# A hybrid streaming trunk: the SSD time-step chain laid token by token on 128 partitions, with the first B tile projected ahead of the time steps

## The reference

```python
h = rmsnorm(x, g_pre)
proj = jnp.einsum('bld,de->ble', h, w_in)          # 5648 columns; the last 16 are dt_raw
u, v, za, zb, xbc, dt_raw = jnp.split(proj, EVEN_SPLITS, axis=-1)
...
xbc, new_ctx = causal_dwconv(xbc, conv_ctx, conv_w, conv_b)   # 4 taps
xbc = jax.nn.silu(xbc)                              # 1024 columns x, 256 B, 256 C
dt = jax.nn.softplus(dt_raw + dt_bias)              # 16 heads
a = -jnp.exp(a_log)
acs = jnp.cumsum(dt * a, axis=2)                    # restarts in every block of 128 tokens
...
decay = jnp.exp(jnp.where(causal[:, :, None, None], seg, -jnp.inf))   # seg = acs_l - acs_s
to_end = jnp.exp(acs[:, :, -1:] - acs)
blk_decay = jnp.exp(acs[:, :, -1])
y_state = jnp.einsum('bclgn,bcgrpn,bclgr->bclgrp', cm, s_prev, jnp.exp(acs))
```

## Time and profile before

| | us |
|---|---|
| median of three runs | 1663.06 |
| the profiled execution | 1661.99 |
| its span, first to last instruction | 1660.2 |
| TensorE busy | 1576.7 (95%) |
| VectorE busy | 813.7 (49%) |
| ScalarE busy | 668.9 (40%) |
| GpSimd busy | 440.5 (27%) |
| mean granted TensorE clock | 0.984 of full speed |

### The profile page before, as it was taken

How to read it: one execution, slowest core, us unless ns; L and a number is a source line. 1 busy time by engine, 2 the same in 40 slices (tenths; PEclk the granted TensorE clock), 3 DMA queues, 4 the chain that set the end, 5 groups by cost and what they waited for, 6 DMA issues and landing times.

```text
span 1660.2 us, 26649 instructions
## 1 busy us (share of the span) xinstructions
PE 1576.7 (95%) x9562; PEld 1454.8 (88%) x9562; DVE 813.7 (49%) x1753; ACT 668.9 (40%) x1243; POOL 440.5 (27%) x267
## 2 busy tenths in 40 slices
PE   5899999998999999999999899999999999998898
PEld 5899999998999999978888788989898889887676
DVE  5755677664885323135565633434433443435432
ACT  6432333232223332334455344444444544445321
POOL 1113444333221121144443221312122221215000
PEclk9999999998999999999999899999999999999999
DMA  4121122212102111053555436523241323213121
GB/s 146 40 66 57 56 70 71 84 43 55 51 25 54 39 39 50 25 178 127 184 175 152 65 64 57 49 51 74 41 70 38 65 41 67 49 50 133 52 89 70
DMA packets 128740, 121.06 MB, mean 73 GB/s; under 512 B 9706, under 2 KB 112500, under 8 KB 128684
## 3 DMA queue, kind: packets, MB, share of 16 engines
q1 hardware_dynamic: 128684, 120.30, 29.6%
HBM read 101.61 MB, written 18.66 MB: 72 GB/s over the span
## 4 chain that ended last, share of the span: by engine, by line
PE 80%; DVE 7%; issue 5%; ACT 5%; DMA 1%; POOL 1%; SPq 0%; ACTq 0%; DVEq 0%; POOLq 0%
PE PB L719 75%; PE PB L723 6%; DVE NRML L1744 2%; ACT L1240 1%; ACT L1630 1%; DMA XS<-in_x_prompt_dram 1%; ACT WH L1234 1%; ACT NRMH L1234 1%; ACT SB L1707 0%; DMA nf_rows<-NFROW 0%; DVE DTROW L1744 0%; ACT PT L1234 0%; DVE XT L1751 0%; DVE KALL L1751 0%; DVE SB L1748 0%
## 5 line engine op out<-in xcount | busy, mean ns | idle before, releaser
L719 PE MATMUL PB<-HH,WH 128*128 128x352 f32 x1872 | 621.5, 332 | 14.9 <-ACT XR L1254 6.0
L719 PE MATMUL PB<-HH,WL 128*128 128x352 f32 x1872 | 605.0, 323 | 0.0
L719 PE MATMUL PB<-HL,WH 128*128 128x352 f32 x1872 | 604.5, 323 | 0.0
L719 PEld LDWEIGHTS PB<-HH,WH 128*128 128x128 f32 x1872 | 355.3, 190 | 28.9 <-issue 20.2
L719 PEld LDWEIGHTS PB<-HL,WH 128*128 128x128 f32 x1872 | 356.1, 190 | 0.0
L719 PEld LDWEIGHTS PB<-HH,WL 128*128 128x128 f32 x1872 | 354.7, 189 | 0.0
L604 POOL TENSOR_TENSOR WL<-WRAW,WH 128x1024 fp32r<-128x1024 f32 x82 | 200.7, 2449 | 564.5 <-ACT WH L1234 556.9
L1234 ACT ACTIVATE WH<-WRAW 128x1024 fp32r<-128x1024 f32 x112 | 117.8, 1052 | 27.5 <-DMA WRAW<-in_w_in_even_dram 19.5
L1707 ACT ACTIVATE SB<-SB,small 128x128 f32<-128x128 f32 (+8 forms) x72 | 53.8, 748 | 80.5 <-DVE small L1748 80.5
L1744 DVE TENSOR_TENSOR Y<-PB,Y 128x128 f32 (+2 forms) x72 | 20.2, 280 | 133.2 <-PE PB L719 133.1
L719 PE MATMUL PB<-PT,VTOK 128*128 128x128 f32 (+2 forms) x624 | 81.9, 275 | 0.1
(11 more groups left out here) (290 smaller groups left out, 2424.1 us busy)
## 6 DMA issues: line engine op xcount, KB each, us to landing
WRAW<-in_w_out_even_dram SPq DMA_DIRECT2D x48, 512.0 KB, 3.5
WRAW<-in_w_in_even_dram SPq DMA_DIRECT2D x44, 512.0 KB, 3.8
WRAW<-in_w_in_odd_dram SPq DMA_DIRECT2D x32, 512.0 KB, 8.1
ACSB<-acs_rows SPq DMA_DIRECT2D x16, 528.0 KB, 4.9
NFB<-nf_rows SPq DMA_DIRECT2D x8, 656.0 KB, 3.7
XS<-in_x_prompt_dram SPq DMA_DIRECT2D x8, 512.0 KB, 5.7
XT<-in_x_prompt_dram SPq DMA_DIRECT2D x8, 512.0 KB, 4.7
x_rows<-OG SPq DMA_DIRECT2D x8, 512.0 KB, 5.3
```

The source lines that it names most:

```text
L719: return pe.matmul(out, lhsT, rhs, start=start, stop=stop)
```

## The change

- Tile order: B0 becomes tile 0, the time-step columns tile 1; B1, C0, C1 stay tiles 2 to 4 (`W_BC = (0, 2, 3, 4)`). SyncE loads B0's weights after the sixth activation tile; the time-step weights come after the convolution weights. `dt_bias` and `a_log` are loaded spread on all partitions.
- The raw time steps are read as 16 rows into `DTRAW` and transposed at once, in nine pieces, behind chunk 0 of B1. From there the chain runs on tiles of 128 partitions x 144 elements (nine blocks times 16 heads): `DTX, DTN, DTE, DTW, DTL, DTC, DTA, DTD`.
- The scan is replaced by a product with a triangle of ones (`TRI`, from `MASKT`), and the block's end by a product with ones, both behind B1. Two transposes of the sums behind chunk 0 of C0 give the rows that are stored, now in nine pieces.
- `TOKQ` is written in place; the 36 transposes, the copies after them and `DECR` are gone.
- ScalarE's order: the readings and the Silu of B0, B1, C0 are placed differently between the chain's steps; `conv_silu(1)` now stands behind the reading of C0.

```diff
-W_DT, W_BC, W_XZ, W_V, W_UZ, W_OE, W_F, W_QKVZ, W_OO = 0, 1, 5, 21, 29, 45, 93, 94, 126
+W_DT, W_XZ, W_V, W_UZ, W_OE, W_F, W_QKVZ, W_OO = 1, 5, 21, 29, 45, 93, 94, 126
+W_BC = (0, 2, 3, 4)
@@ sync
-            if b == 3:
-                load_w(tile_no(W_DT, 1, 0), even(DT0, HEADS_B), HEADS_B)
+            if b == 5:
+                load_w(tile_no(W_BC[0], 1, 0), even(XBC0 + 8 * P))
...
+        load_w(tile_no(W_DT, 1, 0), even(DT0, HEADS_B), HEADS_B)
+        sp.dma_start(DTBB[:, :], dt_bias[0:1, :].broadcast_to([P, HEADS_B])).then_inc(S("par_in"), 16)
+        sp.dma_start(ALB[:, :], a_log[0:1, :].broadcast_to([P, HEADS_B])).then_inc(S("par_in"), 16)
...
-        sp.wait_ge(S("dtc"), 3)
-        sp.dma_start(acs_rows, ACSROW[:, :]).then_inc(S("acs_stored"), 16)
-        sp.wait_ge(S("acs_stored"), 16)
-        sp.wait_ge(S("dt_turn"), 1)
+        sp.wait_ge(S("dt_rows"), 2)
+        for b in range(NB):
+            sp.dma_start(acs_rows[:, b * P:(b + 1) * P], ACSR[b * HEADS_B:(b + 1) * HEADS_B, :]) \
+                .then_inc(S("acs_stored"), 16)
+        sp.dma_start(acs_rows[:, SEQ:TOK], ACSS[:, :]).then_inc(S("acs_stored"), 16)
+        sp.wait_ge(S("acs_stored"), 16 * 9)
@@ tensor
-        for w in range(1, W_XZ):
-            project(tile_no(w, 1, 0), tile_no(w, 1, 0), HH, HL)
-        pe.wait_ge(S("dt_rows"), 1)
-        for i, row in enumerate((RW[0], RW[2], RW[3], ACSROW)):
-            for b in range(NB + 1):
...
-        mm(PB[4][:, 256:256 + 9 * HEADS_B], ONES[0:HEADS_B, :], DECR[:, :, :].rearrange("k h b -> k (h b)")) \
-            .then_inc(S("dt_turn"), 1)
+        project(tile_no(W_DT, 1, 0), tile_no(W_DT, 1, 0), HH, HL)
+        w1 = tile_no(W_BC[1], 1, 0)
+        project_chunk(w1, w1, 0, HH, HL)
+        pe.wait_ge(S("c_read2"), W_DT + 1)
+        pe.wait_ge(S("dtc"), 1)
+        for b in range(NB + 1):
+            last = turn(PB[3][:, b * HEADS_B:(b + 1) * HEADS_B], DTRAW[:, b * P:(b + 1) * P])
+        last.then_inc(S("dt_turn"), 1)
+        project_chunk(w1, w1, 1, HH, HL)
+        project_chunk(w1, w1, 2, HH, HL)
+        pe.wait_ge(S("dtc"), 4)
+        steps = DTA[:, :, :].rearrange("p b h -> p (b h)")
+        mm(PB[4][:, 0:9 * HEADS_B], TRI[:, :], steps)
+        mm(PB[4][:, 256:256 + 9 * HEADS_B], ONES[:, :], steps).then_inc(S("dt_turn"), 1)
+        w2 = tile_no(W_BC[2], 1, 0)
+        project_chunk(w2, w2, 0, HH, HL)
+        pe.wait_ge(S("dtc_a"), 4)
+        turn(PB[3][:, 0:P], TOKQ[:, 3, 0:NB, :].rearrange("p b h -> p (b h)"))
+        turn(PB[3][0:HEADS_B, P:P + DEC], TOKQ[0:DEC, 3, NB, :]).then_inc(S("dt_turn"), 1)
+        project_chunk(w2, w2, 1, HH, HL)
+        project_chunk(w2, w2, 2, HH, HL)
+        project(tile_no(W_BC[3], 1, 0), tile_no(W_BC[3], 1, 0), HH, HL)
@@ scalar
+        read_chunks(tile_no(W_BC[0], 1, 0), parted(XR, 3, SAMP))
+        split_high(tile_no(W_BC[1], 1, 0))
+        dt, raw = tile_no(W_DT, 1, 0), whole(DTRAW, HEADS_B)
+        read_chunk(dt, raw, 0, HEADS_B)
+        read_chunk(dt, raw, 1, HEADS_B)
+        conv_silu(0, BT[:, 0, :])
+        read_chunk(dt, raw, 2, HEADS_B)
+        split_high(tile_no(W_BC[2], 1, 0))
+        load_ln_exp()
...
+        read_chunk(tile_no(W_BC[1], 1, 0), parted(XR, 3, SAMP), 0)
+        act.wait_ge(S("dtc"), 2)
+        act.activation(DTE[:, :, :], DTN[:, :, :], ACT.Exp).then_inc(S("dtc_a"), 1)
+        act.wait_ge(S("dtc"), 3)
+        order(act.activation(DTL[:, :, :], DTW[:, :, :], ACT.Ln))
+        order.fence()
+        act.activation(DTN[:, :, :], DTL[:, :, :], ACT.Exp, scale=-1.0).then_inc(S("dtc_a"), 1)
+        read_chunk(tile_no(W_BC[1], 1, 0), parted(XR, 3, SAMP), 1)
+        read_chunk(tile_no(W_BC[1], 1, 0), parted(XR, 3, SAMP), 2)
+        split_high(tile_no(W_BC[3], 1, 0))
+        act.wait_ge(S("dt_turn"), 2)
+        sums = PB[4][:, 0:9 * HEADS_B].rearrange("p (b h) -> p b h", h=HEADS_B)
+        ends = PB[4][:, 256:256 + 9 * HEADS_B].rearrange("p (b h) -> p b h", h=HEADS_B)
+        order(act.activation(DECB[:, :, :].rearrange("p h b -> p b h"), ends, ACT.Exp))
+        copy(TOKQ[:, 3, :, :], sums).then_inc(S("dtc_a"), 1)
...
+        act.activation(DTE[:, :, :], DTD[:, :, :], ACT.Exp).then_inc(S("dtc_a"), 1)
+        act.wait_ge(S("dt_turn"), 3)
+        copy(ACSR[:, :], PB[3][:, 0:P]).then_inc(S("dt_rows"), 1)
+        copy(ACSS[:, :], PB[3][0:HEADS_B, P:P + DEC]).then_inc(S("dt_rows"), 1)
+        act.wait_ge(S("conv"), 2)
+        read_chunks(tile_no(W_BC[2], 1, 0), parted(XR, 3, SAMP))
+        split_high(tile_no(W_XZ, 1, 0))
+        conv_silu(1, BT[:, 1, :])
+        act.wait_ge(S("conv"), 3)
+        read_chunks(tile_no(W_BC[3], 1, 0), parted(XR, 3, SAMP))
+        split_high(tile_no(W_XZ + 1, 1, 0))
+        conv_silu(2, CT[:, 0, :])
+        conv_silu(3, CT[:, 1, :])
         act.wait_ge(S("conv"), 4)
@@ vector
+        dve.memset(DTRAW[:, TOK:], 0.0).then_inc(S("dtc"), 1)
...
+        conv(0, 8, tile_no(W_BC[0], 1, 0))
...
+        tt(DTA[:, :, :], TOKQ[:, 0, :, :], EALB[:, :, :], ALU.mult).then_inc(S("dtc"), 1)
         dve.wait_ge(S("dtc_a"), 4)
+        ends = PB[4][:, 256:256 + 9 * HEADS_B].rearrange("p (b h) -> p b h", h=HEADS_B)
+        tt(DTD[:, :, :], ends, TOKQ[:, 3, :, :], ALU.subtract).then_inc(S("dtc"), 1)
+        conv(1, 9, tile_no(W_BC[1], 1, 0))
+        dve.wait_ge(S("dtc_a"), 5)
+        tt(TOKQ[:, 1, :, :], DTE[:, :, :], TOKQ[:, 0, :, :], ALU.mult).then_inc(S("tokq"), 1)
```

More of the change, by code:

```diff
@@ L158, in hybrid_trunk @@
     SS, MS, RT, RR = small[:, 0:9], small[:, 9:18], small[:, 18:27], small[:, 27:36]
-    DTB, AL, EAL, BF = small[:, 36:37], small[:, 37:38], small[:, 38:39], small[:, 39:40]
+    BF = small[:, 39:40]
     MX, MXR, NBIAS = small[:, 40:44], small[:, 44:45], small[:, 45:46]
@@ L201, in hybrid_trunk @@
     CSO = r("CSO", [6 * XBC_TILES, P])
-    ACSB = (at("ACSB0", acs_at, [P, TOK]), r("ACSB1", [P, TOK]))
-    r = Region(rows_at, rows_end)
-    RW = [r(f"DTROW{i}", [HEADS_B, TOK]) for i in range(4)]
+    ACSB = (ACSB0, r("ACSB1", [P, TOK]))
     r = Region(A_R5 + 4 * TOK * 4, A_W)
-    RW += [r(f"DTROW{i}", [HEADS_B, TOK]) for i in range(4, 8)]
+    DTRAW = r("DTRAW", [HEADS_B, 9 * P])
+    DTX, DTN, DTE, DTW, DTL, DTC, DTA, DTD = [r(f"DT{n}", [P, 9, HEADS_B]) for n in "XNEWLCAD"]
+    EALB = r("EALB", [P, 9, HEADS_B])
+    DTBB, ALB, EAL = [r(n, [P, HEADS_B]) for n in ("DTBB", "ALB", "EAL")]
+    TRI = r("TRI", [P, P])
+    ACSR = r("ACSR", [P, P])
+    ACSS = r("ACSS", [HEADS_B, DEC])
     YB = at("YB", A_R5, [P, 8, TOK])
@@ L1311, in log1p_exp_steps, with read_chunk @@
             act.activation(neg, lg, ACT.Exp, scale=-1.0).then_inc(S(name + "_a"), 1)
-        read_chunks(tile_no(W_DT, 1, 0), whole(RW[4], HEADS_B), rows=HEADS_B)
-        split_high(tile_no(W_DT + 2, 1, 0))
+        def read_chunk(w, outs, c, rows=P):
+            act.wait_ge(S("p_chunk"), times(w, 3, c + 1))
+            for cols, out in outs[c]:
+                last = copy(out, PB[c][0:rows, cols])
+            last.then_inc(S(f"c_read{c}"), 1)
+        read_chunks(tile_no(W_BC[0], 1, 0), parted(XR, 3, SAMP))
@@ L1315, in _ @@
+        split_high(tile_no(W_BC[1], 1, 0))
[5 more added lines that the diff above has]
+        split_high(tile_no(W_BC[2], 1, 0))
         load_ln_exp()
-        log1p_exp_steps(RW[5][:, :], RW[6][:, :], RW[1][:, :], RW[2][:, :], "dtc")
         act.wait_ge(S("par_in"), 64)
-        act.activation(EAL[0:HEADS_B, :], AL[0:HEADS_B, :], ACT.Exp).then_inc(S("dtc_a"), 1)
@@ L1319, in _ @@
[L1319 to L1337, removed]
+        act.activation(EAL[:, :], ALB[:, :], ACT.Exp).then_inc(S("dtc_a"), 1)
@@ new lines, in _ @@
+        split_high(tile_no(W_BC[3], 1, 0))
[4 more added lines that the diff above has]
+        copy(TOKQ[:, 3, :, :], sums).then_inc(S("dtc_a"), 1)
+        order.fence()
+        act.wait_ge(S("dtc_a"), 4)
+        order(act.activation(TOKQ[:, 2, :, :], TOKQ[:, 3, :, :], ACT.Exp))
@@ new lines, in _ @@
+        order.fence()
+        act.wait_ge(S("dtc"), 5)
+        act.activation(DTE[:, :, :], DTD[:, :, :], ACT.Exp).then_inc(S("dtc_a"), 1)
[6 more added lines that the diff above has]
+        conv_silu(1, BT[:, 1, :])
@@ L1821, in log1p_exp @@
             order.fence()
[L1823 to L1828, removed]
+        dve.memset(DTRAW[:, TOK:], 0.0).then_inc(S("dtc"), 1)
+        order(dve.memset(EALB[:, :, :], 0.0))
+        dve.wait_ge(S("masks"), 1)
+        order(ts(TRI[:, :], MASKT[:, :], 0.0, None, ALU.is_ge))
@@ new lines, in _ @@
+        conv(0, 8, tile_no(W_BC[0], 1, 0))
+        dve.wait_ge(S("dtc_a"), 1)
+        order.fence()
+        order(ts(EALB[:, 0:NB, :], EAL[:, :].unsqueeze(1).broadcast_to([P, NB, HEADS_B]), -1.0, None, ALU.mult))
+        order(ts(EALB[0:DEC, NB, :], EAL[0:DEC, :], -1.0, None, ALU.mult))
+        dve.wait_ge(S("dt_turn"), 1)
+        turned = PB[3][:, 0:9 * HEADS_B].rearrange("p (b h) -> p b h", h=HEADS_B)
+        order(tt(DTX[:, :, :], turned, DTBB[:, :].unsqueeze(1).broadcast_to([P, 9, HEADS_B]), ALU.add))
```

(25 more changed lines are left out.)

15 lines of the change are left out of this document (4 added, 11 removed).

## The result

The changed kernel took 1654.77 us (median of 5 runs, 1653.39 to 1655.68) against 1663.37 us for the kernel before beside it: 8.6 us less, ratio 0.9948, 95% interval 0.9933 to 0.9962. On another chip the same two kernels came to 1655.9 and 1664.74 us, 8.8 us apart, ratio 0.9948 (0.9936 to 0.9960). 9.4 us had been forecast.

A forecast was written before the change was run, and what follows sets the result against it. TensorE, holding 80% of the chain, was taken to bound the kernel. Removing 11.50 us, adding 1.4 on TensorE and 0.7 in the head, gave 9.4 us less: a median of 1653.7 us, range 1651.8 to 1658.8.

The forecast's parts named there:

- The gap and its clock, 5.98 + 1.44: TensorE's idle wait before the matmul at 74.58, 5.98 us, and ten low-clock matmuls behind it, 1.44 us, go away.
- The old transposes and their clock, 2.49 + 1.59: TensorE's 36 transposes and decay product from 99.11, 2.49 us, and eleven low-clock matmuls behind, 1.59 us, go away.
- the rival that kept those 1.59 us: Second low clock on TensorE not from the transposes, so 1.59 us come back elsewhere: 1655.3 us; chance 0.05.
- The new groups, 1.4: Nine transposes, triangle and ones products, and two transposes of sums add 1.4 us on TensorE; bounds 1.0 and 2.5.
- The rival with the clock falling at them: TensorE's clock falls at the new small groups, 1.5 us each; two give 1656.7 us; chance 0.08.
- The chain, 3.5 us, and its cover: Thirteen VectorE and ScalarE steps before the triangle product, 0.27 us each, 3.5 us, hidden with 4.1 us of cover.
- The slow-chain rival: VectorE steps before the triangle product cost 2.0 us each, chain 23 us, TensorE waits 15.4: 1670.5 us; chance 0.05.
- The conv links: Conv of B1 or C0 comes 3 us late, TensorE waits 1.2 us and more before C1: 1655 to 1657; chance 0.07.
- The head, 0.7: TensorE's start comes 0.7 us later: B0's earlier load costs 1.57 us, 0.8 us saved; bounds 0 and 1.6.
- the credit: In the head, moving the time-step weights' 64-byte rows later saves 0.8 us of DMA time between 7 and 9 us.
- The late time-step tile: In the head, time-step weights land at 25.3 where ScalarE wants them at 19.9, 5.4 us lost: 1659.1; chance 0.07.

The follow-up runs named there:

- before_exp_late: The kernel before with ScalarE's two Exp of the time steps moved behind its reading of B1: 1662.2 us against 1663.15, ratio 0.9997.
- turns_36: The changed kernel with each of the nine 16-row transposes done four times, 36 in a row: 1657.27 us, ratio 0.9958 to the kernel before.
- chain_8_more: The changed kernel with eight 128 x 1152 memsets on VectorE before the time-step chain's last step: 1663.37 us, ratio 0.9999 to the kernel before.

## Why the prediction was right, step by step
- **The gap and its clock, 5.98 + 1.44.** Gone, as said; before_exp_late shows that the chain made them.
- **The old transposes and their clock, 2.49 + 1.59.** Gone. That the clock's fall belonged to them was argued; turns_36 now shows it, and with it the rival that kept those 1.59 us is out.
- **The new groups, 1.4.** The stretch shrank from 78.51 to 68.33, 10.2 us, where 11.50 − 1.4 = 10.1 was said. The rival with the clock falling at them is out.
- **The chain, 3.5 us, and its cover.** The chain ran from the transposes' end (63.6) to 67.3, 3.7 us; TensorE came to the product at 71.27, 3.9 us later. VectorE's steps on 128 x 144 took 0.24 and 0.31 us, where 0.27 was said; ScalarE's 0.33:
```profile
63.63 0.31 DVE L1788 TENSOR_TENSOR DTX<-PB,DTBB 128x144 f32<-128x144 f32 x1 [0.44 <-PE PB L729]
63.98 0.24 DVE L1792 TENSOR_SCALAR DTN<-DTX 128x144 f32<-128x144 f32 x1
...
67.03 0.31 DVE L1788 TENSOR_TENSOR DTA<-TOKQ,EALB 128x144 f32<-128x144 f32 x1
```
  The slow-chain rival, the one that would have ended slower, put the point where the gain is spent at 15.6 us; with the 10.4 us of chain_8_more on top of 3.7 it was 14.1, and the time was that of the kernel before. The point came 1.5 us early, as the loss at the low clock was 0.8 us more than charged and the whole gain 0.8 us less than forecast.
- **The conv links.** Conv of B1 was over at 80.5. Its last three steps, with no split beside them, took 4.04 us, as did those of C0 and C1, and as three times the lower price of the earlier trace rows gives. The wait for GpSimd showed in a place I had not thought of, a copy of three elements behind the start of a `split_low` (VectorE's, then GpSimd's timeline):
```profile
73.65 1.78 DVE L1829 COPY XR<-COLS 128x3 f32<-128x3 f32 x1
...
76.48 4.04 DVE L1795 SCALAR_TENSOR_TENSOR ACC<-XR,CONVW,ACC 128x1059 f32<-128x1059 f32 x3
...
73.02 2.40 POOL L610 TENSOR_TENSOR WL<-WRAW,WH 128x1024 fp32r<-128x1024 f32 x1 [9.98 <-ACT WH L1252]
```
- **The head, 0.7.** This is the term that was mis-sized: on ScalarE it was 1.4 us. Of its two parts the credit failed, the 0.8 us for the 64-byte rows that no longer stood ahead of the last tiles. I had taken it that the queues would then move 800 KB between 7 and 9 us, where they had moved 482. Windows of the changed kernel, columns as in the earlier trace rows:
```profile
7.00:8.00 1.00, 0.00 (x0) 0.00 (x0) 0.00 (x0) 1.00 (x1) 0.00 (x0) 1.00 1.00 311
8.00:9.00 1.00, 0.34 (x1) 0.18 (x1) 0.61 (x2) 0.99 (x3) 0.00 (x0) 1.00 0.87 295
```
  They moved 606 KB, 124 more, which at 410 GB/s is 0.3 us and not 0.8. With the 1.57 us for B0's bytes that makes 1.3 us, near the 1.4; this sum is an estimate, as no run has the one part without the other. Around the last full tile, which landed at 17.87, the rate falls again:
```profile
14.00:15.00 1.00, 1.00 (x5) 1.00 (x6) 0.81 (x3) 0.21 (x3) 0.00 (x0) 1.00 1.03 403
15.00:16.00 1.00, 1.00 (x7) 1.00 (x6) 0.20 (x1) 0.00 (x0) 0.00 (x0) 1.00 1.37 192
16.00:17.00 1.00, 1.00 (x7) 1.00 (x6) 0.00 (x0) 0.59 (x1) 0.00 (x0) 1.00 1.59 93
```
  But the kernel before has the same dip around its last full tile, though its 64-byte rows had landed at 9.4 us, so these rows are not shown to be what made the changed head later:
```profile
14.00:15.00 1.00, 1.00 (x7) 1.00 (x6) 0.77 (x2) 1.00 (x3) 0.00 (x0) 1.00 1.16 182
15.00:16.00 1.00, 1.00 (x6) 1.00 (x5) 0.96 (x3) 0.49 (x2) 0.00 (x0) 1.00 1.21 114
```
  The Trainium skill ("DMA: Bandwidth & Descriptors", Specifications) has 512 bytes as the size from which a transfer runs at line rate. The windows of both kernels agree, with 403 and 410 GB/s for full tiles and 93 to 192 where small pieces stand behind the last one, the 16-byte rows of the convolution weights in both.
  On TensorE the head is harder to read. Between the unchanged pairs the projection starts 1.6 us later (37.9 against 36.4), over all ten traces with these two heads 0.8 us (37.5 against 36.7). The 10.2 us less either makes 8.6 to 9.4: the 8.6 and 8.8 measured lie at one end, the 9.4 forecast at the other. So the 0.7 us between forecast and result fits this term, but the scatter of the heads could make as much.
- **The late time-step tile.** SyncE was held 3.79 us in its issue, as the rival had it, but by the profile it landed 8.4 us after that issue's start at 10.60, at 19.0 us, and ScalarE, later itself, did not wait. Out.

## What to carry to other kernels
When an engine reads in program order and sits at a wait, first ask what the waited-for chain costs on its own engine: reordering alone moved a 6 us wait by one tile, a chain with 144 elements a partition instead of 1056 removed it. Groups of narrow work on TensorE are best kept apart by full projections: 27 more narrow transposes cost 3.2 us in one piece, with the clock's fall, and 2.6 us in three groups, without it. And when a load is moved in a queue that paces the start, work out from the windows what the freed stretch will really move, and look at which tile the load now stands ahead of.
